# A two-layer decoder trunk: block 1's GLA gate product moved behind the first gathers, its weights loaded in eight idle pieces

## What is computed

```python
# layer 0 mixer: one input projection, split into stick-breaking heads and GLA heads
p = rmsnorm(x) @ w_in
q_sb, k_sb, v_sb, q_g, k_g, v_g, g_g, a_lr = split(p)
o_g = gla(q_g, k_g, v_g, log_a)
o_g = rms(o_g) * gla_norm * silu(g_g)          # g_g: the gate product
x = x + concat(stick_breaking(q_sb, k_sb, v_sb), o_g) @ w_out
# every layer: PEER
q = rmsnorm(x) @ w_q                            # 8 heads, two halves each
scores = q . subkeys ; top 16 + top 16 -> 256 sums -> best 16 = 16 expert numbers per head
out = sum_k softmax(best)_k * gelu(u_tab[id_k] . x) * v_tab[id_k]
```

## Time and profile before

| | us |
|---|---|
| median of 3 runs | 1607.27 |
| lowest, highest | 1605.94, 1607.56 |
| the profiled execution | 1605.99 |
| its span | 1604.3 |
| PE busy | 1427.8 (89%) |
| DVE busy | 978.4 (61%) |
| ACT busy | 670.0 (42%) |
| POOL busy | 654.7 (41%) |
| mean DMA rate over the span | 390 GB/s |

### The profile page before, as it was taken

The page is one execution under the profiler, slowest core; times in us unless marked ns, Lnnn a source line. Parts: engine busy times, 40 slices in busy tenths (PEclk is TensorE's granted clock), DMA queues, the critical chain, the costliest instruction groups (busy, mean ns, idle before and its releaser), DMA issues.

```text
span 1604.3 us, 14828 instructions
## 1 busy us (share of the span) xinstructions
PE 1427.8 (89%) x4442; PEld 702.9 (44%) x4442; DVE 978.4 (61%) x2484; ACT 670.0 (42%) x1851; POOL 654.7 (41%) x535
## 2 busy tenths in 40 slices
PE   7999989999958888998988899999999889797776
PEld 6656445565413334443443445355335345242222
DVE  1225578748748666653446756566456677777744
ACT  1514544534525334342344534343344454444433
POOL 1002344544424333343435433333334544456673
PEclk9999999999989999999999999999999999999999
DMA  7325999999999999999999999999999999999996
GB/s 291 131 105 192 405 415 388 422 421 421 421 422 421 420 422 422 421 417 421 422 416 416 399 411 421 421 421 403 422 421 409 423 420 410 422 421 421 422 422 276
DMA packets 86512, 625.53 MB, mean 390 GB/s; under 512 B 9744, under 2 KB 9888, under 8 KB 10656
## 3 DMA queue, kind: packets, MB, share of 16 engines
q0 software_dynamic: 73728, 536.90, 81.1%
q1 hardware_dynamic: 12528, 87.40, 13.4%
q10 hardware_dynamic: 176, 0.28, 0.0%
HBM read 623.50 MB, written 1.05 MB: 389 GB/s over the span
## 4 chain that ended last, share of the span: by engine, by line
PE 43%; DMA 35%; DVE 9%; ACT 5%; issue 4%; POOL 3%; SPq 0%; POOLq 0%; DVEq 0%; ACTq 0%
DMA ring<-in_peer_uv,experts 34%; PE acc L1619 23%; PE work L1399 5%; DVE ring L1275 5%; PE work L1382 4%; POOL ring L704 3%; PE work L1371 3%; PE acc L1582 1%; ACT diag L908 1%; ACT gelus L906 1%; PE work L1475 1%; PE work L1426 1%; PE acc L1413 1%; ACT L905 1%; ACT gelus L905 1%
## 5 line engine op out<-in xcount | busy, mean ns | idle before, releaser
L1619 PE MATMUL acc<-ring,diag 128*128 128x512 f32 x2048 | 979.1, 611 | 157.7 <-ACT diag L908 155.7
L704 POOL DMA_INDIRECT ring<-in_peer_uv,experts x512 | 645.2, 1260 | 846.2 <-PE acc L1619 697.3
L1275 DVE CUSTOM_DVE_ANT_0 ring<-ring,h 128x1024 f32<-128x1024 f32 x512 | 624.7, 1225 | 437.1 <-DMA ring<-in_peer_uv,experts 424.2
L1619 PEld LDWEIGHTS acc<-ring,diag 128*128 128x128 f32 x2048 | 368.3, 192 | 687.5 <-ACT diag L908 347.7
L905 ACT ACTIVATE gelus<-dots 128x1 f32<-128x1 f32 x512 | 103.3, 202 | 690.9 <-DVE dots L1275 688.7
L908 ACT ACTIVATE diag<-ident,gelus 128x128 f32<-128x128 f32 x512 | 205.5, 401 | 16.7
L906 ACT ACTIVATE gelus<-gelus,gates 128x1 f32<-128x1 f32 x512 | 150.8, 294 | 16.6
L1399 PEld LDWEIGHTS work<-hT,weights 128*128 128x128 f32 x512 | 63.3, 192 | 18.2 <-issue 18.2
L1382 PE MATMUL work<-weights,hT 128*128 128x512 f32 x152 | 70.5, 592 | 0.0
L1399 PE MATMUL work<-hT,weights 128*128 128x128 f32 x512 | 63.6, 275 | 0.0
L905 ACT ACT_TABLE_LOAD x41 | 52.6, 1283 | 0.7
(11 more groups left out here) (242 smaller groups left out, 942.4 us busy)
## 6 DMA issues: line engine op xcount, KB each, us to landing
weights<-in_c_w_in SPq DMA_DIRECT2D x14, 1024.0 KB, 15.9
weights<-in_peer_w_q SPq DMA_DIRECT2D x9, 1024.0 KB, 8.1
weights<-in_ab_w_in SPq DMA_DIRECT2D x8, 1024.0 KB, 6.0
ring<-in_peer_uv,experts POOLq DMA_INDIRECT x512
weights<-in_c_w_out SPq DMA_DIRECT2D x7, 1024.0 KB, 12.3
more<-in_c_w_in SPq DMA_DIRECT2D x6, 1024.0 KB
x<-in_c_w_in SPq DMA_DIRECT2D x5, 1024.0 KB
weights<-in_ab_w_out SPq DMA_DIRECT2D x4, 1024.0 KB, 5.2
```

What stands on the lines that cost most here:

```text
L704: pool.indirect_dma_start(ring[:, t % SLOTS, :], None, uv_rows, bass.IndirectOffsetOnAxis(ap=experts[:, b, step:step + 1], axis=0))\
L1275: nc.vector.tensor_tensor_reduce(out=ring[:, k, 0:D], in0=ring[:, k, 0:D], in1=h[:, b, :], scale=1.0, scalar=0.0, op0=ALU.mult, op1=ALU.ad ...
L1619: last = nc.tensor.matmul(acc[2 * b + n][:, :], diag[:, k, :], ring[:, k, D + n * CH:D + (n + 1) * CH], start=False, stop=True, skip_group ...
```

## The change

1. `GG` of block 1 leaves its place between `KD` and `GS` and stands behind `LOG` of batches 2 to 5, just ahead of `STICKE` 2. By then the room of its weights in `weights` would be in use, so the 2 MB go, right behind the loads of `GQ`, into eight pieces that are idle then (seven DMAs: one of 512 KB into `h`, six of 256 KB into `more`, `ring` and `mixT`). Both `GG` products read them there (`gate_values`). One piece lies in slot 5 of the ring, so gather 5 now waits for `GG` of block 1. `GG` takes no chunk of `weights` any more, so `w_out`'s first chunk gets the room that is free earlier.
2. The queries and scores of head 1 for block 0 (`QPROD`, `QMORE`, `QTAKE`, `QDOT`, `DTAKE` with heads (1,)) leave their place ahead of `STICKE` and stand behind steps 0 to 3.
3. Head 1's ranking starts behind step 4 rather than 0, with a spacing of 1.4 steps, so that its last part stands behind step 11 rather than 5.
4. Block 1's `SOUT` stands behind step 3 rather than 0, and the GLA norm, `GLAT` and `GLATAKE` behind 4 to 8. Its eight `OUT` quarters stand behind 6, 8, 10, 18, 20, 22, 24, 26 rather than 2 to 9, `OADD` behind 27 rather than 10, the norm behind 28 to 30 rather than 11 to 13, `TRANSPOSE` behind 36 rather than 15.
5. The query tiles of heads 2 and 3 stand behind 12, 13, 15, 16 rather than 12 to 15, those of heads 4 and 5 start at 28 with a spacing of 1.9 rather than 27 with 2. `SPATIAL` 9 (was 6), `CAUSAL` 22 (was 20).

```diff
-           ("GG", 0), ("KD",), ("GG", 1), ("GS",), ("GV", 0), ("QKEYS", 0), ("WOUT",), ("SOUT", 0), ("STAKE", 0), ("KV", 0),
+           ("GG", 0), ("KD",), ("GS",), ("GV", 0), ("QKEYS", 0), ("WOUT",), ("SOUT", 0), ("STAKE", 0), ("KV", 0),
...
-        + [("SOFTLN", 2, 3, 4, 5), ("GV", 1), ("PROJV", 1), ("LOG", 2, 3, 4, 5)] + scored(0, 0, 0, (1,))[:-1]
-        + [("STICKE", 2), ("STICKE", 3), ("KV", 1), ("QDOT", 0, 0, 0, (1,)), ("DTAKE", 0, 0, 0, (1,)),
+        + [("SOFTLN", 2, 3, 4, 5), ("GV", 1), ("PROJV", 1), ("LOG", 2, 3, 4, 5), ("GG", 1), ("STICKE", 2), ("STICKE", 3), ("KV", 1),
...
-    out = [(0, ("SOUT", 1)), (1, ("STAKE", 1)), (1, ("GLASTAT", 1)), (2, ("GLAMEAN", 1)), (3, ("GLAOUT", 1)),
-           (4, ("GLAT", 1)), (5, ("GLATAKE", 1)), (6, ("SPATIAL",)), (20, ("CAUSAL",))]
-    out += [(step, ("OUT", 1, n, q)) for n, steps in enumerate(((2, 3, 6, 7), (4, 5, 8, 9))) for q, step in enumerate(steps)]
-    out += ranked(0, 0, 0, 1) + [(10, ("OADD", 1))] + normed(11, "ffn0", 1)
-    out += [(15, ("TRANSPOSE", (1,), "ffn0")), (16, ("HTAKE", (1,), "ffn0"))]
-    return (out + projected(12, 0, 0, 1, 1) + ranked(20, 0, 0, 2) + ranked(26, 0, 0, 3)
+    second = (0, 0, 0, (1,))
+    out = [(0, ("QPROD", *second)), (1, ("QMORE", *second, 1)), (2, ("QTAKE", *second)), (2, ("QDOT", *second)),
+           (3, ("DTAKE", *second)), (3, ("SOUT", 1)), (4, ("STAKE", 1)), (4, ("GLASTAT", 1)), (5, ("GLAMEAN", 1)),
+           (6, ("GLAOUT", 1)), (7, ("GLAT", 1)), (8, ("GLATAKE", 1)), (9, ("SPATIAL",)), (22, ("CAUSAL",))]
+    out += [(step, ("OUT", 1, n, q)) for n, steps in enumerate(((6, 8, 10, 18), (20, 22, 24, 26))) for q, step in enumerate(steps)]
+    out += ranked(4, 0, 0, 1, 1.4) + [(27, ("OADD", 1))] + normed(28, "ffn0", 1)
+    out += [(36, ("TRANSPOSE", (1,), "ffn0")), (37, ("HTAKE", (1,), "ffn0"))]
...
+                        elif t == 5:
+                            n = BANKS["GG", 1]
+                            pool.wait_ge(full[n % WB], n // WB + 1)
...
+            def gate_values(n, b):
+                w = claim_bank(pe, n)
+                pe.wait_ge(gg_chunk_in, 16 * (KT - 1))
+                for k in range(KT):
+                    last = nc.tensor.matmul(w[:, :], hT[:, k, b * P:(b + 1) * P], gg_chunk[k],
+                                            start=(k == 0), stop=(k == KT - 1))
+                last.then_inc(full[n % WB], 1)
```

More of the change, by code:

```diff
@@ L72, in chunks_of @@
         return int(layer == 1 or (b == 0 and not first_chunk_holds(layer, m)))
-    if kind in ("GG", "GV"):
-        return int(kind == "GG" and args[0] == 0)
     return {"PROJQK": 2, "GQ": 1, "WOUT": 2, "ZPROJ": 1, "MIXO": 2}.get(kind, 0)
@@ L141, in ranked @@
 def ranked(at, layer, b, hd, gap=1):
-    out = [(at + gap * part, ("TOPK", layer, b, hd, part)) for part in range(TK_PARTS)]
-    return out[:4] + [(at + gap * 4, ("GEXP", layer, b, hd))] + out[4:]
+    out = [(int(at + gap * part), ("TOPK", layer, b, hd, part)) for part in range(TK_PARTS)]
+    return out[:4] + [(int(at + gap * 4), ("GEXP", layer, b, hd))] + out[4:]
 def normed(at, name, b):
@@ L209, in parts_of_layer0 @@
 def parts_of_layer0():
[L211 to L217 removed]
+    second = (0, 0, 0, (1,))
[5 more added lines that the diff above has]
+    out += [(36, ("TRANSPOSE", (1,), "ffn0")), (37, ("HTAKE", (1,), "ffn0"))]
+    return (out + projected(12, 0, 0, 1, 1.5) + ranked(20, 0, 0, 2) + ranked(26, 0, 0, 3)
+            + projected(28, 0, 0, 2, 1.9) + ranked(38, 0, 0, 4, 2) + projected(38, 0, 1, 1, 5) + ranked(50, 0, 0, 5, 2)
             + projected(56, 0, 1, 2, 3) + projected(68, 0, 0, 3, 1.5) + ranked(77, 0, 0, 6) + projected(76, 0, 1, 0, 4)
@@ L358 @@
     BANKS[_kind, *_args] = _at.bank
+    if _kind == "WOUT":
+        OUT_CHUNK = _at.chunk
     if _kind == "QPROD":
@@ L447, in trunk @@
         gv_chunk = slots(4, 4).rearrange("p (k n) -> p k n", n=CH)
+        gg_chunk = ([h[:, 1, k * CH:(k + 1) * CH] for k in range(2)] + [more_rows[:, k * D + CH:(k + 1) * D] for k in (2, 3)]
+                    + [slots(11)[:, k * CH:(k + 1) * CH] for k in range(2)]
+                    + [mixT[:, k:k + 4, P:T] for k in (0, 4)])
         kz = slots(8, 2).rearrange("p (j t) -> p j t", t=T)
@@ L499, in trunk @@
         gv_chunk_in = sem("gv_chunk_in")
+        gg_chunk_in = sem("gg_chunk_in")
         v_chunk_in = [sem(f"v_chunk_in{k}") for k in range(2)]
@@ L597, in _ @@
                         sp.dma_start(gv_chunk[:, k * KT // 2:(k + 1) * KT // 2, :], ab_w_in[4][:, k * KT // 2:(k + 1) * KT // 2, :]).then_inc(gv_chunk_in, 16)
-                elif kind == "GG" and args[0] == 0:
-                    load_chunk(chunk, ab_w_in[5], 2 * [filled(BANKS["GG", 1])])
+                    sp.wait_ge(*filled(at.banks["TRANSPOSE", (0, 1), "mix0"] + 3))
+                    sp.dma_start(h[:, 1, :], ab_w_in[5][:, 0:2, :].rearrange("p k n -> p (k n)")).then_inc(gg_chunk_in, 16)
+                    for k in range(2, KT):
+                        src = ab_w_in[5][:, k, :]
+                        if k >= 6:
+                            src = src.rearrange("p (a t) -> p a t", t=P)
+                        sp.dma_start(gg_chunk[k], src).then_inc(gg_chunk_in, 16)
                 elif kind == "WOUT":
@@ L1554, in _ @@
                 elif kind == "GG":
-                    tall(bank, chunk - args[0], hT, args[0])
+                    gate_values(bank, args[0])
                 elif kind == "GV":
@@ L1579, in _ @@
                     own_copies(BANKS["GLAT" if q >= 2 else "SOUT", b], 1)
-                    wt = await_chunk(pe, at.chunk - 2 + n, (q // 2,))
+                    wt = await_chunk(pe, OUT_CHUNK + n, (q // 2,))
                     for k in range(q * KT // 4, (q + 1) * KT // 4):
```

## The result

| | before | changed |
|---|---|---|
| median, us | 1606.88 (22 runs) | 1609.30 (22 runs) |
| lowest to highest | 1605.22 to 1610.18 | 1606.43 to 1612.38 |
| ratio of the times, 95% interval | | 1.0013 (1.0007 to 1.0019) |
| profiled execution, span | 1605.99, 1604.3 | 1611.43, 1609.7 |

The time is inside the range, and the change is within 0.2%. But the sum said 0.3 us faster and the kernel is 2.4 us **slower**, and the interval excludes zero. That difference has a cause, and the experiments look for it.

A forecast was written before the change was run, and what follows sets the result against it. It took bytes at 421 GB/s to set the end, through the position reached by 274 us, with compute holding transfers before. Terms -6.9, +2.9, +4.1 and -0.4 gave -0.3 us: median 1607.0, range 1601.5 to 1611.0.

The forecast's parts named there:

- The start and steps 0 to 11: From gather 0 to gather 16: gather 0 goes 6.87 us earlier, but the lead is gone at 190.4 us.
- the wait for gather 16: Gather 16 waits for head 1's numbers until 188.4 us, and the transfers stand idle for some 4 us.
- Table loads: On ACT: each load takes 1.28 us with no drain behind it, so at the gate's sigmoid nothing is lost.
- The compute of steps 12 to 26: Head 2's ranking begins at 215.3 us instead of 220.02, and its numbers come at 230.5 instead of 235.12.
- The transfers have ... to fill 190.4 to 250.2: 20 gathers and 4 MB of weights fill this stretch; the kernel before did the same with 0.4 us lost.
- Add and norm in the ranking: Between head 2's and head 3's numbers: block 1's add and norm add 5.8 us to 16.9 us.
- The slower rival: Add and norm in head 3's ranking: the add waits 4.9 us, not 0.6, giving 1611.3 us; chance 0.18.
- Its threshold of 3.8 us: DVE's wait at block 1's residual add from which the slower case decides, 3.2 us more than forecast.
- PE and DVE need less than 2.49 us a step: From step 38 on: the plan is the same and compute stays under one gather's 2.49 us a step.
- weights later and the norm in the ranking -0.4: Last term of the sum, for the stretch behind 190 us: 0.4 us gained.

The follow-up runs named there:

- e7: The changed kernel with nothing of the GLA norm within head 1's ranking, and SOUT, the GLA norm, SPATIAL and the first OUT quarters later: 1611.59 us, ratio 1.0030.
- e1: The changed kernel measured and profiled again with no edit: 1609.62 us, ratio 1.0013 to the kernel before.
- e13: The kernel before with only block 1's add behind step 27, norm behind 28 to 30, transpose behind 36 and 37: 1606.98 us, ratio 0.9999.
- e5: The changed kernel with block 1's add behind step 32, norm behind 33 to 35, transpose behind 37, one query tile a step later: 1608.23 us, ratio 1.0003.
- e12: The kernel of e5 run once more, against the kernel before: 1606.53 us, ratio 0.9994.
- e4: The changed kernel with block 1's OUT quarters behind steps 5 to 12, add behind 13, norm behind 14 to 16, transpose behind 18: 1607.73 us, ratio 1.0003.

## Why the prediction failed, step by step

**The start and steps 0 to 11** held. `GG` out of PE's path moved gather 0 by 6.65 us; gather 5 was released by the gate product (line 1496 in the issues above); gather 16 was released by `experts` after POOL had been idle for 7.86 us. DVE waited 8.17 us for the scores, 1.99 at `GLAMEAN` and 2.70 at `GLATAKE`. The rate from 130 to 190 was 325 against 323: the lead was gone at 190, as forecast. I took the wait for gather 16 as the place of the loss; e7 shows PE's work behind it as the next bound, close behind.

**Table loads** cost what the rows gave. ACT in e1:

```profile
244.24 1.28 ACT L764 ACT_TABLE_LOAD   x1
245.53 0.20 ACT L764 ACTIVATE roots<-roots 128x1 f32<-128x1 f32 x1
245.75 1.28 ACT L918 ACT_TABLE_LOAD   x1
247.05 0.20 ACT L918 ACTIVATE gelus<-dots 128x1 f32<-128x1 f32 x1
```

A load of 1.28 us, and the next operation 0.01 us behind it. The Trainium skill ("ScalarE: Activation LUTs", What ACT_TABLE_LOAD costs) puts a drain of about 1.38 us there; by it two loads would have cost 2.8 us more, and no run here shows that.

**The compute of steps 12 to 26** held: head 2's ranking began at 215.41 (215.3 forecast) and its numbers came at 230.51 (230.5).

**"The transfers have ... to fill 190.4 to 250.2"** failed: 409 GB/s, not 418, or 1.3 us. I had set only the sum of the bytes against the time, and took the rate to be full from 190.4 on. It was full only from 198 on (424 and more up to 210): 317 GB/s from 190 to 194 and 367 from 194 to 198, together 1.5 us, and a further 0.4 us from 210 to 218 (410 and 387). The first of these windows:

```profile
190.00:194.00 4.00, 4.00 (x10) 1.71 (x9) 3.32 (x7) 3.23 (x11) 2.83 (x3) 1.00 0.90 317
```

Gathers 16 to 18 go out within 2.6 us, but gathers 19 and 20 wait for products 11 and 12 on PE (193.66 and 195.38), and the `OUT` quarter behind 10 stands ahead of both. Before, the rate was 428 and 430 in these windows. PE's matmuls of e1 from 190 to 250 by line, then before (count, busy us, mean ns; one product or quarter shows as 4 matmuls):

```profile
L1640 PE MATMUL acc<-ring,diag 128*128 128x512 f32 x76 | 35.6, 601 | 3.7 <-ACT diag L921 3.4
L1603 PE MATMUL acc<-weights,mixT 128*128 128x512 f32 x23 | 10.8, 592 | 0.0
```

```profile
L1619 PE MATMUL acc<-ring,diag 128*128 128x512 f32 x85 | 40.3, 604 | 6.0 <-ACT diag L908 5.8
...
L1582 PE MATMUL acc<-weights,mixT 128*128 128x512 f32 x4 | 1.9, 592 | 0.0
```

In 60 us PE did 23 matmuls of `OUT` instead of 4 and 76 of the products instead of 85, some two products fewer. From gather 20 to 24 the issues are 3 us apart, over the 2.49 us of a transfer. That cost nothing at once, but is a likely reason for the 0.4 us from 210 to 218; no run takes out these quarters alone.

**Add and norm in the ranking** was the mis-sized term. I took 5.8 us; from head 2's to head 3's numbers e1 took 254.27 - 230.51 = 23.76 us against 16.9, so 6.8. The missing 1.0 us is the longer wait for the last quarter (1.35 instead of 0.6) and for `VEC` (2.06 instead of 1.78). (The terms that I listed add up to 5.2, not 5.8; two small operations on `roots`, 0.3 us together, stood in no term.) e13, with the quarters done by then, needs 21.33 us, 4.4 more. The slower rival named this place rightly, with a wait of 4.9 us; the wait was 1.35. Its threshold of 3.8 us was set so that this wait alone would cost 3.2 us; I gave smaller waits no weight, and 1.0 us here stands beside two more terms of that size. What the whole step was worth e5 and e12 tell: with add and norm behind the ranking the changed kernel is 2.2 us faster.

**"PE and DVE need less than 2.49 us a step" from step 38 on** failed as well. PE was busy 29.78 of 30 us from 274 to 304. The transpose that the change puts behind step 36 falls into PE's full stretch, in e1 at 268.70, and the wait for the next diagonal with it:

```profile
268.70 1.04 PE L1340 MATMUL work<-ident,h 128*128 128x128 f32 x8
269.58 1.88 PE L1640 MATMUL acc<-ring,diag 128*128 128x512 f32 x4
271.91 1.95 PE L1640 MATMUL acc<-ring,diag 128*128 128x512 f32 x4 [0.45 <-ACT diag L921]
```

About 0.9 + 0.45 = 1.3 us; the rate from 274 to 304 is 409 instead of 423, 1.0 us. I had counted the transpose as moved and asked for no cover. This attribution is argued from the rows: gathers 44 to 46 take 5.0 us in e1 and in e13, 3.45 in the kernel before and in e4, whose transpose stands elsewhere. But in e5 the transpose stands only one step later and the rate from 274 to 304 was 422, so it seems to cost time only where the transfers have nothing ahead.

The sum as measured, e1 against before: 190 and earlier -0.3, to 250 +1.3, to 274 -0.7, to 304 +1.0, together +1.3 us. Gather 60 is 1.96 us later and the span 2.0 us longer, so some 0.7 us are in no window of mine; they stay open. **The failed term of my sum** so is the last one, "weights later and the norm in the ranking -0.4": in its place stand +1.6 us from 190 to 304 by the rates, and with the 0.7 us that no window shows some +2.3, while the stretch ahead of 190 came as forecast. Open is also how the 2.4 us between e13 and the changed kernel divide between late queries, GLA norm and late quarters: no run undid one without the others at these places.

## What to carry to other kernels

A lead at the start is worth only what the fullest engine behind it lets through (e7: 9.0 us ahead at gather 16, 0.4 at gather 24): add up each engine's work from the new start to the point where the rate is full for good, not only the waits. A step moved out of one wait (DVE's 6.18 us at step 10) gains only if its new place is off every chain: here inside a ranking it was a draw, behind it a gain of 1.7 us with five numbers of the plan changed. And a transfer stream with few buffers needs each issue in time, not only enough bytes in the stretch.

## What the runs showed of the hardware that was not expected

The first projection, 128 matmuls of the same kernel, took 27.88 us in some executions and 29.5 to 30.1 in others, with the granted clock given as 1.00 in both. The difference lies in its first 4 us, where the slow execution did 10 matmuls and the other 19. PE in the windows of 2 us, first in the kernel before (27.86 us), then in the changed kernel's profiled execution (29.81 us):

```profile
12.00:14.00 2.00, 1.69 (x8) 1.00 1.03 434
14.00:16.00 2.00, 2.00 (x11) 1.00 1.01 409
```

```profile
12.00:14.00 2.00, 1.69 (x4) 1.00 0.98 414
14.00:16.00 2.00, 2.00 (x6) 1.00 1.03 420
```

The granted clock can fall in one execution and not in another at the same place. In the changed kernel's profiled execution PE stood idle for 2.84 us, and the four matmuls and the tile behind took 2.57 and 3.06 us; in e1 the same idle time of 2.84 us was followed by 1.98 and 1.95. The windows of these places, first the profiled execution, then e1:

```profile
244.00:248.00 4.00, 4.00 (x14) 2.66 (x13) 3.86 (x14) 3.37 (x8) 0.96 (x1) 0.62 1.01 416
```

```profile
242.00:246.00 4.00, 4.00 (x22) 2.78 (x22) 3.86 (x12) 3.37 (x8) 0.94 (x1) 1.00 1.02 422
```

A mean of 0.62 means that most of that window was at 1.2 GHz and the rest at 2.4. It cost 0.6 + 1.1 = 1.7 us there, as much as gather 60, set back, is later in this execution than in e1 (1.7 us).
